# Attention's probability transposes moved into the stop of the values and the scores

## What is computed

```
s = einsum('bqkgd,bskd->bkgqs', qg, k) * HEAD_DIM ** -0.5     # scores
p = softmax(s)                                                # C: mask, and a sink logit in the sum
o = einsum('bkgqs,bskd->bqkgd', p, v)                         # values
```

## Time and profile before

| | us |
|---|---|
| median of 3 runs | 1484.71 (1484.25 to 1486.94) |
| the profiled execution | 1486.11 |
| its span, first to last instruction | 1484.4 |
| TensorE busy | 1438.8 (97%) |
| VectorE busy | 870.6 (59%) |
| ScalarE busy | 589.2 (40%) |
| GpSimd busy | 177.6 (12%) |
| mean granted TensorE clock | 0.99 of full speed |

### The profile page before, as it was taken

The page is one execution under the profiler, slowest core; times in us unless marked ns, Lnnn a source line. Parts: engine busy times, 40 slices in busy tenths (PEclk is TensorE's granted clock), DMA queues, the critical chain, the costliest instruction groups (busy, mean ns, idle before and its releaser), DMA issues.

```text
span 1484.4 us, 26130 instructions
## 1 busy us (share of the span) xinstructions
PE 1438.8 (97%) x9053; PEld 1378.3 (93%) x9053; DVE 870.6 (59%) x1609; ACT 589.2 (40%) x1082; POOL 177.6 (12%) x173
## 2 busy tenths in 40 slices
PE   5999999999999999998998999999999999999998
PEld 4899999998988999998988999999999989999998
DVE  3776666543444877776776866665453674455433
ACT  3544454532333433332244454544332453333322
POOL 2220020111222000000012201101131300000000
PEclk7999999999999999999999999999999999999999
DMA  9732123256766555547663322242344724332341
GB/s 312 217 121 86 57 86 114 86 180 204 222 217 198 185 184 178 190 152 244 212 189 107 115 86 67 80 132 91 104 130 139 255 86 142 125 129 90 114 131 50
DMA packets 208909, 215.58 MB, mean 145 GB/s; under 512 B 7897, under 2 KB 202777, under 8 KB 208665
## 3 DMA queue, kind: packets, MB, share of 16 engines
q1 hardware_dynamic: 178616, 168.50, 36.1%
q10 hardware_dynamic: 29760, 44.57, 9.1%
q0 software_dynamic: 416, 1.05, 0.2%
HBM read 211.98 MB, written 2.11 MB: 144 GB/s over the span
## 4 chain that ended last, share of the span: by engine, by line
PE 76%; DVE 8%; issue 7%; ACT 3%; ACTq 2%; DMA 2%; DVEq 0%; POOL 0%; POOLq 0%
PE bank L759 23%; PE bank L760 22%; PE bank L761 22%; DVE unread L1422 4%; ACT w_hi L1074 3%; PE tr L928 2%; PE sc L904 2%; PE tr L913 2%; DVE w_lo L1316 2%; PE sc L830 1%; PE tr L860 1%; DVE ff_f L1348 1%; ACTq L629 1%; DMA mod_t<-in_w_mod_t 1%; ACTq L636 1%
## 5 line engine op out<-in xcount | busy, mean ns | idle before, releaser
L759 PE MATMUL bank<-h_hi,w_lo 128*128 128x384 f32 x1664 | 568.3, 342 | 10.9 <-DVE h_lo L1321 6.9
L761 PE MATMUL bank<-h_hi,w_hi 128*128 128x384 f32 x1664 | 558.4, 336 | 0.0
L760 PE MATMUL bank<-h_lo,w_hi 128*128 128x384 f32 x1664 | 558.1, 335 | 0.0
L1316 DVE TENSOR_TENSOR w_lo<-raw,w_hi 128x1024 fp32r<-128x1024 f32 (+3 forms) x352 | 385.0, 1097 | 294.1 <-ACT w_hi L1074 293.9
L1074 ACT CAST w_hi<-raw 128x1024 fp32r<-128x1024 f32 (+3 forms) x352 | 322.4, 922 | 130.6 <-PE bank L761 108.3
L759 PEld LDWEIGHTS bank<-h_hi,w_lo 128*128 128x128 f32 x1664 | 313.8, 189 | 23.2 <-issue 12.5
L760 PEld LDWEIGHTS bank<-h_lo,w_hi 128*128 128x128 f32 x1664 | 314.0, 189 | 0.0
L761 PEld LDWEIGHTS bank<-h_hi,w_hi 128*128 128x128 f32 x1664 | 313.7, 189 | 0.0
L759 PE MATMUL bank<-br_hi,w_lo 128*128 128x384 f32 (+1 forms) x384 | 131.9, 343 | 3.3 <-DVE br_lo L1322 3.3
L761 PE MATMUL bank<-br_hi,w_hi 128*128 128x384 f32 (+1 forms) x384 | 128.6, 335 | 0.0
L760 PE MATMUL bank<-br_lo,w_hi 128*128 128x384 f32 (+1 forms) x384 | 128.4, 334 | 0.0
(11 more groups left out here) (191 smaller groups left out, 1292.0 us busy)
## 6 DMA issues: line engine op xcount, KB each, us to landing
raw<-in_w_in SPq DMA_DIRECT2D x120, 512.0 KB, 4.6
raw<-in_w_gate_up SPq DMA_DIRECT2D x88, 512.0 KB, 4.4
raw<-in_w_down SPq DMA_DIRECT2D x48, 384.0 KB, 3.7
mod_t<-in_w_mod_t ACTq DMA_DIRECT2D x34, 512.0 KB, 3.4
raw<-in_w_branch SPq DMA_DIRECT2D x64, 256.0 KB, 3.7
mod_w<-in_w_mod ACTq DMA_DIRECT2D x32, 512.0 KB, 4.9
raw<-in_w_out SPq DMA_DIRECT2D x16, 512.0 KB, 4.5
start_w<-in_w_mod SPq DMA_DIRECT2D x12, 512.0 KB, 8.7
```

The source lines that it names most:

```text
L759: pe.matmul(out, w[1], r[0], start=start, stop=False)
L760: pe.matmul(out, w[0], r[1], start=False, stop=False)
L761: return pe.matmul(out, w[0], r[0], start=False, stop=stop)
L1316: dve.tensor_tensor(to, src, hi.bitcast(F32), ALU.subtract).then_inc(lo_ready.sem, 1)
```

## The change

The list of steps is laid out anew: an even step holds `probsT(j-1), attn(j-2), scores(j)`, an odd step only `scale(j)`, and one empty step goes ahead of the list (44 steps instead of 43). So TensorE does the three in one stop. The results of `attn` move to columns 384 to 511 of both banks of `tr`, beside the transposes, so that the values no longer wait for ScalarE's copy of the transposes just made; instead ScalarE's copy waits for `attn_out` of the step before (the values in the same stop). `reader` becomes a list of signals for each bank. For step 0 the copy also waits for the last split of the queries, which lies in the same memory as `prob_t`.

```diff
@@ plan()
         if k % 2 == 0:
+            now += [("probsT", j - 1)] if 1 <= j <= NA else []
             now += [("attn", j - 2)] if j >= 2 else []
             now += [("scores", j)] if j < NA else []
         else:
             now += [("scale", j)] if j < NA else []
-            now += [("probsT", j - 1)] if j >= 1 else []
         steps.append(now)
+    steps = [[]] + steps
@@ attn_bank(i)
             n = len(attention_step(i)[1])
-            return tr[:, 0, 512 - P * n:512].rearrange("p (c q) -> p c q", c=n)
+            return tr[:, 0:n, 3 * P:4 * P]
@@ claim(b), on TensorE
-                if reader.get(b):
-                    pe.wait_ge(*reader[b])
+                for done in reader.get(b, ()):
+                    pe.wait_ge(*done)
@@ hook "probsT", on TensorE
-                    reader[0] = reader[1] = probs_t_ready(l, i)
+                    reader[0], reader[1] = [probs_t_ready(l, i)], [probs_t_ready(l, i)]
@@ hook "attn", on TensorE
-                    claim(0)
-                    reader[0] = attn_ready(l, i)
+                    for b in range(len(cs)):
+                        if i < NA - 1:
+                            reader[b].append(attn_ready(l, i))
+                        else:
+                            claim(b)
+                            reader[b] = [attn_ready(l, i)]
                     tiles = (0, 1, 2) if t < 2 else (3,)
                     for n in range(len(cs)):
-                        to = slice(512 - P * (len(cs) - n), 512 - P * (len(cs) - n) + P)
                         for b, v in enumerate(tiles):
                             for g in range(2):
-                                ins = pe.matmul(tr[64 * g:64 * g + 64, 0, to], vals[:, m, v, 64 * g:64 * g + 64],
+                                ins = pe.matmul(tr[64 * g:64 * g + 64, n, 3 * P:4 * P], vals[:, m, v, 64 * g:64 * g + 64],
                                                 prob_t[:, i % 2, g, b + n, :], start=b == 0, stop=v == tiles[-1])
@@ hook "probsT", on ScalarE
                     act.wait_ge(*probs_turned(l, i))
+                    if i == 0:
+                        act.wait_ge(*qk_split(l, 9))
                     if i == 1:
                         act.wait_ge(*kv_stored(l, 0))
-                    if i >= 2:
-                        act.wait_ge(*attn_out(l, i - 2))
+                    if i >= 1:
+                        act.wait_ge(*attn_out(l, i - 1))
```

More of the change, by code:

```diff
@@ L862, in hook @@
                     ins.then_inc(q_stat.sem, 1)
-                    reader[1] = q_mixed(l, i)
+                    reader[1] = [q_mixed(l, i)]
                 elif what == "rnorm":
@@ L872, in hook @@
                     ins.then_inc(q_bcast.sem, 1)
-                    reader[0] = k_ready(l, i)
+                    reader[0] = [k_ready(l, i)]
                 elif what == "vt":
@@ L879, in hook @@
                     ins.then_inc(v_turned.sem, 1)
-                    reader[0] = v_ready(l, i)
+                    reader[0] = [v_ready(l, i)]
                 elif what == "kout":
@@ L884, in hook @@
                     pe.transpose(tr[:, 0, 0:P], q_mix[:, i, CTX], ident).then_inc(k_turned.sem, 1)
-                    reader[0] = k_out_ready(l, i)
+                    reader[0] = [k_out_ready(l, i)]
                 elif what == "cache":
@@ L889, in hook @@
                     pe.transpose(tr[:, 0, 0:P], k_past[:, i, :], ident).then_inc(past_turned.sem, 1)
-                    reader[0] = past_split(l, i)
+                    reader[0] = [past_split(l, i)]
                 elif what == "scores":
@@ L985, in _ @@
                 reader.clear()
-                reader[1] = tail_ready(l, -1)
+                reader[1] = [tail_ready(l, -1)]
                 for n in range(0, 3):
```

## The result

The changed kernel is slower: 1501.51 us, the median of 4 runs (1497.91 to 1502.08), against 1484.62 us in the same call. The ratio is 1.0112, with an interval of 1.0099 to 1.0124. Five later runs (e_after_again) gave 1498.66 us and 1.0106 [1.0088, 1.0125]. The medians lie 16.9 us apart in the first and 14.1 us in the second. The profiled run took 1502.08 us with a span of 1500.4, at 0.988 of the full clock.

A forecast was written before the change was run, and what follows sets the result against it. TensorE alone was taken to bound the attention stretches. From the profiled 1486.1 us, less 3.4 for lost restarts, plus 15.4 of waits, came 1498.1; the median lying 1.4 lower, 1496.7 us was forecast, range 1486 to 1503.

The forecast's parts named there:

- The bound: In both layers' attention stretches TensorE alone sets the time, so whatever it does more, or waits, is paid in full.
- What it adds: waits: TensorE's transposes come due before VectorE has scaled the probabilities: 7.7 us a layer, 15.4 in all.
- step 4: Attention step with pooling between scores and scaling: probabilities after 7.9 us, transposes due after 7.0, a wait of 0.9 us.
- The due times of 6.3 and 8.4 us: Time from scores' end until TensorE reaches the transposes, with 12 or 16 chunks of products between.
- the later start on the scores of 0.5 us: VectorE's maximum begins 0.5 us after the scores, behind ScalarE's copy and the values' split; bounds 0 and 0.8.
- step 11: Attention step with two full splits in the lag: wait 0.7 us, plus about 0.9 as VectorE is late after step 10.
- What it removes: The transposes' own stop vanishes: 0.09 us of restart each, 19 x 2 times, a gain of 3.4 us.
- the seam of transposes and values: New tile change in the merged stop, taken as 0.10 us over the pitch, bounds 0 and 0.25 us.
- In time after all: Rival: transposes find their probabilities ready, only the 3.4 us gain shows, 1481.3 us; chance 0.08.
- Half of it: Rival: the 0.5 us behind the copy is hidden, waits 2 us a layer, 1485.3 us, no change; chance 0.14.
- A stop costs more than its restart: Rival: each vanished stop gives back 0.25 us, 9.5 in all, with waits as forecast, 1490.6 us; chance 0.08.
- Waits feed waits: Rival: late scalings delay VectorE's next work and GpSimd's sums double some, 12 us a layer, 1505 us; chance 0.14.

The follow-up runs named there:

- e_after_again: The changed kernel once more, unaltered, in five rounds beside the kernel before: 1498.66 us, ratio 1.0106.
- e_values_first: Against the changed kernel, ScalarE writes the high part of the values first and copies the transposes behind it: 1493.57 us.
- e_far: Against the changed kernel, the merged stop takes the transposes of step i-2 and the values of step i-3, so later after their scores: 1486.0 us.
- e_no_shift: The changed kernel without the empty step ahead of the list, 43 steps instead of 44: 1505.22 us.
- e_old_layout: The changed kernel with its new list, but transposes and values sharing columns as before, so values wait for the copy: 1534.17 us.
- e_dose_after: The changed kernel with one more VectorE pass over the probabilities (times 1.0) ahead of the scaling: 1518.54 us.

## Why the prediction was right, and where it was not

**The bound.** Right: every wait of TensorE in the stretch came out as time. Between the same products a layer takes 7.28 us more. The waits make 6.91 of it. The rest, 0.4 us, is the restart behind a wait: transposes that had to wait run 0.80 to 0.81 us to the values instead of 0.75, eight times a layer.

**What it adds: waits.** Right in mechanism, place and size, but for the reason given at step 4. Forecast 7.7 us a layer, 7.2 in eight named steps and 0.5 in four others; measured 6.91 in those eight and nothing in the four. The due times of 6.3 and 8.4 us were measured as 6.29 and 8.37, the later start on the scores of 0.5 us as 0.58, the handover of 0.06 us as 0.05 to 0.06, the longest waits were at steps 17 and 11, as said. Of the difference of 0.8 us, 0.5 are the four steps taken as late. They are in time by 0.2 to 0.8 us. Most of the rest is step 11: what step 10's late scaling passes on to it is some 0.6 us and not 0.9.

**Step 4: right size, wrong reason.** I had given it the lag and the copy's 0.5 us. With the copy moved (e_values_first) its scaling ended no earlier. What sets the lag there is the split of the pooled result ahead of the scaling, and that stands until TensorE has done its own pooling products. The copy's delay is swallowed by it. That 0.9 and 0.79 us lie so near is luck. At steps 7 and 11 the copy's delay doesn't count either, since VectorE is late for the scores by itself.

**What it removes: the step that failed.** The term of the sum was 19 x 2 x 0.09 = 3.4 us gain. A merged stop measures 2.39 us against 2.40 for the two, and e_far, with the merged stops and no waits, is 0.5 us longer in its stretches than the kernel before, not 3.4 shorter. The gain is nothing that can be measured. The mis-sized part is the seam of transposes and values, taken as 0.10 us over the pitch. It is 0.74 from start to start less 0.57 for six transposes: 0.17 us, which the weight loads' row shows too (6.9 us in 40). The bounds given, 0 to 0.25, held it. The restart behind the lone transposes is really gone, and the seam behind the same transposes costs 0.07 us more than was put for it, which takes most of it back. The prediction named a seam clearly off 0.1 us as a sign of being wrong. For this term it is one; the time stayed in its range because the term is small beside the waits. The Trainium skill, in "TensorEngine Tiling (Array Packing)", Key Properties, has a change of tiling mode drain TensorE. The idle 0.17 us at each such seam agrees with it, and merging took away no change of mode.

**The rivals.** "In time after all" fell to the waits. "Half of it" fell too: the 0.5 us behind the copy is not hidden in five of eight steps. "A stop costs more than its restart" is contradicted by the 2.39 us of the stop and by e_far, which has the merged stop and no waits and gains nothing. "Waits feed waits" is real at step 11 alone, at 0.6 us a layer; e_no_shift shows how another place of the same list takes the kernel there (1505.22 us), with the scaling at 2.00 us beside GpSimd, the mechanism that this rival named, and with a half clock behind the hole, which no rival had named.

**The sum.** Forecast +15.4 and -3.4, so +12.0. Measured: +13.8 for waits, +0.9 for the restarts behind them, which the forecast didn't have, and nothing for the merging: 14.7 us, where the stretches grew by 14.6. The waits were forecast 1.6 us too high; the gain that didn't come (3.4 us) and the restarts left out (0.9 us) work the other way, so the two errors partly cancel. The profiled runs' spans lie 16.0 us apart; 1.8 of that is the late start. The medians' 16.9 and 14.1 us lie on both sides of 14.6, and what parts them isn't explained further.

## What to carry to other kernels

Before moving work that another engine feeds nearer to its source, take the lag from the trace (here scores to scaled probabilities, 6.3 to 9.3 us), compare it step by step with the new due time, and add what the move itself puts into the feeding queues. Look in the lag for waits on the engine that is to be served, as at step 4: they set it whatever is moved elsewhere. A stop between products costs its restarts and its changes of tile; count both, since merging two stops that keep every change of tile saved nothing measurable of 2.40 us. Slack that is spent costs nothing until it is gone, and then each microsecond counts in full: the same extra pass on VectorE cost 2.7 us before the change and 17 to 20 after it. A long hole can cost more than its length, as the half clock of e_no_shift shows.

## What the runs showed of the hardware

The seam from transposes (tile 128x128) to products of tile 128x64 is dearer over the pitch than the one from 384-column products to the same tile, 0.17 against 0.10 us, although the idle of the weight loads before it is shorter (0.17 against 0.25 us). Why is not settled; no run varied it by itself.

A chain TensorE, ScalarE's copy of 0.80 us, TensorE costs 1.05 us over a stop without the wait (e_old_layout), 1.3 times the copy.

Behind holes of 3.24 and 3.25 us TensorE's granted clock was 0.51 and 0.50, until 192.5 and 946.8 us (e_no_shift). The length of the hole alone doesn't decide it. Behind one of 2.79 us (e_dose_after, to 192.86 us) the granted clock was 1.00. In the same kernel it was 0.50 from 993.2 to 996.6 us, behind a hole of 1.77 us, and in e_old_layout from 140.8 to 144.2 us, behind one of 2.15 us.

The first weights' products begin between 34.6 and 38.0 us in kernels that are alike up to there, so a difference of 2 us between single profiles can be nothing but the start.
